# Rounded three-pass latent products, shared low parts and a reordered MLP norm in a hybrid GLA and MLA layer kernel

## The reference

```python
D_MODEL = SEQ = 1024; GLA_HEADS, GLA_DK, GLA_DV = 4, 64, 128; MLA_HEADS = 8; D_FF = 4096
h = _rmsnorm(x, attn_norm[l])
z = h @ w_in[l]
zq, zk, zv, zgate, zg, zcq, zckv, zkpe = jnp.split(z, split_pts, axis=-1)
gate_logit = (zgate @ w_gate_up[l] + b_gate[l]).astype(jnp.float32)
log_a = jnp.maximum(jax.nn.log_sigmoid(gate_logit) / GLA_GATE_NORMALIZER, GLA_LOG_GATE_MIN)
o_gla = _gla_chunked(gq, gk, gv, log_a)            # chunked scan, chunk 64
o_gla = _rmsnorm(o_gla, gla_out_norm[l]) * jax.nn.silu(zg)
q  = (_rmsnorm(zcq,  q_a_norm[l])  @ w_uq[l])      # 256 -> 8 heads x 96
kv = (_rmsnorm(zckv, kv_a_norm[l]) @ w_ukv[l])     # 128 -> 8 heads x 128
# head norms, rotary part of 32, block-causal softmax attention
x = x + jnp.concatenate([o_gla, o_mla], axis=-1) @ w_out[l]
h = _rmsnorm(x, mlp_norm[l])
x = x + jnp.square(jax.nn.relu(h @ w_up[l])) @ w_down[l]
```

## Time and profile before

| | us |
|---|---|
| median of 3 runs | 1159.03 (1159.02 to 1159.75) |
| the profiled execution | 1160.03 |
| its span in the trace | 1158.1 |
| PE busy | 1126.1 (97%) |
| DVE busy | 786.6 (68%) |
| POOL busy | 529.6 (46%) |
| ACT busy | 468.7 (40%) |

### The profile page before, as it was taken

The page is one execution under the profiler, slowest core; times in us unless marked ns, Lnnn a source line. Parts: engine busy times, 40 slices in busy tenths (PEclk is TensorE's granted clock), DMA queues, the critical chain, the costliest instruction groups (busy, mean ns, idle before and its releaser), DMA issues.

```text
span 1158.1 us, 15248 instructions
## 1 busy us (share of the span) xinstructions
PE 1126.1 (97%) x5582; PEld 899.3 (78%) x5582; DVE 786.6 (68%) x1092; ACT 468.7 (40%) x891; POOL 529.6 (46%) x429
## 2 busy tenths in 40 slices
PE   5999999999999999999999999999999999999998
PEld 5977677776766768887788888888887888888887
DVE  5575776637777772157488755775798888988863
ACT  5343544315565562056423223322434344344341
POOL 2352442514344363235844444444536565564562
PEclk9998999999999999999999999999999999999999
DMA  7332242372212114323334334331589784466642
GB/s 244 88 110 64 81 149 81 91 224 63 74 33 60 51 38 153 120 92 128 108 112 161 110 127 143 112 109 72 200 288 340 257 296 147 131 188 216 203 120 89
DMA packets 98346, 158.42 MB, mean 137 GB/s; under 512 B 9248, under 2 KB 38960, under 8 KB 98272
## 3 DMA queue, kind: packets, MB, share of 16 engines
q1 hardware_dynamic: 96720, 152.53, 40.0%
q10 hardware_dynamic: 1008, 3.67, 0.9%
q0 software_dynamic: 544, 1.24, 0.6%
HBM read 115.46 MB, written 41.94 MB: 136 GB/s over the span
## 4 chain that ended last, share of the span: by engine, by line
PE 83%; DVE 9%; issue 3%; POOL 2%; ACT 1%; DMA 1%; SPq 0%; ACTq 0%; DVEq 0%; POOLq 0%
PE ps L1808 78%; PE ps L2043 2%; PE ps L1880 1%; DVE g_cum L1375 1%; DVE t_all L1580 1%; DVE t_new L1580 1%; DVE dr_lo L1580 1%; POOL wi_lo L753 1%; DMA gain<-in_attn_norm_dram 1%; DMA up_raw<-in_w_up_dram 1%; PE ps L1823 0%; PE ps L1945 0%; DVE stage L1580 0%; DVE m_qk L1349 0%; DVE m_nm L1525 0%
## 5 line engine op out<-in xcount | busy, mean ns | idle before, releaser
L1808 PE MATMUL ps<-dr_hi,dl_hi 128*128 128x512 f32 x448 | 174.5, 390 | 1.6 <-DVE dr_lo L1580 1.6
L1808 PE MATMUL ps<-dr_hi,dl_lo 128*128 128x512 f32 x448 | 174.3, 389 | 0.0
L1808 PE MATMUL ps<-dr_lo,dl_hi 128*128 128x512 f32 x448 | 174.3, 389 | 0.0
L882 POOL TENSOR_TENSOR ua_lo<-up_raw,ua_hi 128x1024 fp32r<-128x1024 f32 x46 | 116.8, 2541 | 118.3 <-ACT ua_hi L918 118.3
L904 POOL TENSOR_TENSOR dl_lo<-l_raw,dl_hi 128x512 fp32r<-128x512 f32 x64 | 101.5, 1610 | 70.2 <-ACT dl_hi L918 69.8
L1808 PE MATMUL ps<-wi_hi,a_hi 128*128 128x512 f32 (+1 forms) x256 | 105.9, 414 | 5.3 <-POOL wi_lo L753 3.8
L1808 PE MATMUL ps<-a_hi,ua_hi 128*128 128x512 f32 x256 | 99.9, 390 | 2.0 <-ACT u_two L918 1.8
L904 POOL TENSOR_TENSOR dl_lo<-s_all,dl_hi 128x512 fp32r<-128x512 f32 x48 | 75.0, 1582 | 58.4 <-ACT dl_hi L918 57.7
L1808 PEld LDWEIGHTS ps<-dr_hi,dl_hi 128*128 128x128 f32 x448 | 84.1, 188 | 20.3 <-issue 2.8
L1808 PE MATMUL ps<-a_lo,ua_hi 128*128 128x512 f32 x256 | 99.6, 389 | 0.0
L1808 PE MATMUL ps<-a_hi,ua_lo 128*128 128x512 f32 x256 | 99.6, 389 | 0.0
(11 more groups left out here) (218 smaller groups left out, 2422.9 us busy)
## 6 DMA issues: line engine op xcount, KB each, us to landing
r_raw<-in_w_down_dram SPq DMA_DIRECT2D x144, 256.0 KB, 3.4
hidden<-stage SPq DMA_DIRECT2D x72, 256.0 KB, 2.1
up_raw<-in_w_up_dram SPq DMA_DIRECT2D x16, 1024.0 KB, 5.5
l_raw<-hidden SPq DMA_DIRECT2D x64, 256.0 KB, 3.3
raw<-in_w_in_dram SPq DMA_DIRECT2D x24, 256.0 KB, 3.0
z_gla<-z_stage SPq DMA_DIRECT2D x16, 256.0 KB, 2.0
raw<-in_w_out_dram SPq DMA_DIRECT2D x16, 256.0 KB, 6.7
xs<-in_x_dram SPq DMA_DIRECT2D x8, 512.0 KB, 7.2
```

The costliest lines, as they stand in the source:

```text
L882: pool.tensor_tensor(ua_lo[n % UP_RING][:, :, :], up_source(g, product), ua_hi[n % UP_RING][:, :, :].bitcast(F32), ALU.subtract).then_inc( ...
L1808: return pe.matmul(dst, lhsT, rhs, start=start, stop=stop, skip_group_check=onto)
```

## The change

1. The latents' factors are split too: `c_hi` is ACT's copy, `c_lo` a multiply-and-subtract of DVE (three of 128x128 per block); the weights `m_uq` (128x1536) and `m_ukv` (128x1024) get high parts from ACT and low parts from DVE once, around step 8. The products behind HEADS become three one-pass matmuls each.
2. START becomes 7, 9, ... 21: HEADS falls on odd steps, both transposes on even ones. The head transposes come five steps after START for all blocks, and GATE_T and LOGITS one step earlier.
3. The gates are worked in place in `g_cum`: the lower bound goes into the bias step, the absolute value and a subtraction are dropped, and the sums go behind steps 27 and 28.
4. DVE makes the low parts of tiles 3, 5 and 7 of groups 1 to 3, ahead of `tile_out` of the last step of the group before.
5. `m_ukv` is loaded later, behind the last tiles of group 1.
6. In the MLP norm POOL makes the root of position 4 and 6 ahead of T4's low part, the low parts of T1 to T3 one position later in its list, and `up_low(0, P5)` ahead of three low parts of the last position; ACT makes T4's last high part after `first_parts(1, P1)`.

```diff
-        START = [6, 8, 11, 13, 16, 18, 20, 22]
+        START = [7 + 2 * b for b in range(NB)]
-        HEADS_T_AT = [at_step + (6 if b < NB // 2 else 5) for b, at_step in enumerate(START)]
+        HEADS_T_AT = [at_step + 5 for at_step in START]
-        GATE_T, LOGITS = NB + 1, NB + 3
+        GATE_T, LOGITS, GATE_SUMS = NB, NB + 2, 3 * NB + 3
+        def low_by_vector(n):
+            return KT <= n < KT * IN_GROUPS and n % KT in (3, 5, 7)
+        def low_made(n):
+            of_vector = sum(low_by_vector(m) for m in range(n + 1))
+            return (wlo_done2, of_vector) if low_by_vector(n) else (wlo_done, n + 1 - of_vector)
...
 # SP
-                    sp.wait_ge(wlo_done, KT * q + k - RING + 1)
+                    sp.wait_ge(*low_made(KT * q + k - RING))
...
-                    sp.dma_start(m_ukv[:, :], w_ukv[0]).then_inc(mla_w_in, 16)
                 for b in range(NB - 1):
                     stores(NB * q + b)
                 if q + 1 < IN_GROUPS:
                     for k in range(RING + 2, KT):
                         in_piece(q + 1, k)
+                    if q == 0:
+                        sp.dma_start(m_ukv[:, :], w_ukv[0]).then_inc(mla_w_in, 16)
...
 # POOL
                         for k in range(0, 2) if b == 0 else range(2, KT):
-                            in_low_part(q + 1, k)
+                            if not low_by_vector(KT * (q + 1) + k):
+                                in_low_part(q + 1, k)
...
             for pos in range(NB):
+                if pos >= 2 and late(pos - 2):
+                    t_low(pos - 2, range(3))
                 pool.wait_ge(ssq_ready, NB + pos + 1)
                 rsqrt(rstd[:, 1, pos:pos + 1], ssq[:, 1, pos:pos + 1], D, rstd_ready)
-                if pos >= 1 and late(pos - 1):
-                    t_low(pos - 1, range(3 if pos == NB - 1 else 4))
+                if pos >= 2 and late(pos - 2):
+                    t_low(pos - 2, (3,))
+            t_low(NB - 2, range(3))
             pool.wait_ge(ulo_done, 2)
             up_low(1, P1)
             t_low(NB - 2, (3,))
             t_low(NB - 1, (0,))
             up_low(1, P2)
-            t_low(NB - 1, (1, 2))
             up_low(0, P5)
-            t_low(NB - 1, (3,))
+            t_low(NB - 1, (1, 2, 3))
...
 # ACT
-                        last = copy(m_cT[:, i, :], ps[:, 3, i * P:(i + 1) * P], ga[:, i:i + 1])
+                        last = copy(c_hi[:, i, :], ps[:, 3, i * P:(i + 1) * P], ga[:, i:i + 1])
-                    step(act.activation(g_cum[:, :, :], g_log[:, :, :], ACT.Abs))
...
                 behind(b)
+            act.wait_ge(mla_w_in, 32)
+            copy(m_uq_hi[:, :, :], m_uq[:, :, :]).then_inc(mla_hi, 1)
+            copy(m_ukv_hi[:, :], m_ukv[:, :]).then_inc(mla_hi, 1)
             for q in range(1, IN_GROUPS):
...
             for n, (g, product) in enumerate(UP_ORDER):
                 if product in (P1, P5) and n >= 1:
                     first_parts(g, product)
+                if n == 2:
+                    t_high(NB - 1, (3,))
...
-                if n == 1:
-                    t_high(NB - 1, (3,))
...
 # DVE
-                step(stt(g_log[:, t, :], g_log[:, t, :], 0.0, g_cum[:, t, :], ALU.min, ALU.subtract))
-                step(dve.tensor_scalar(g_log[:, t, :], g_log[:, t, :], 1.0 / GATE_NORM, LOG_GATE_MIN, ALU.mult, ALU.max))
+                step(dve.tensor_scalar(g_cum[:, t, :], g_cum[:, t, :], -1.0 / GATE_NORM, LOG_GATE_MIN, ALU.mult, ALU.max))
...
+                b = prep(s, LATENTS_T)
+                if b is not None:
+                    dve.wait_ge(cT_out, b + 1)
+                    for i in range(3):
+                        last = stt(c_lo[i][:, :], ps[:, 3, i * P:(i + 1) * P], ga[:, i:i + 1], c_hi[:, i, :].bitcast(F32),
+                                   ALU.mult, ALU.subtract)
+                    last.then_inc(clo_done, 1)
...
+            def in_low_parts(q):
+                for k in range(KT):
+                    n = KT * q + k
+                    if low_by_vector(n):
+                        dve.wait_ge(whi_done, n + 1)
+                        dve.tensor_tensor(wi_lo[:, n % SLICES, :], raw[:, k % RING, :], wi_hi[:, n % SLICES, :].bitcast(F32),
+                                          ALU.subtract).then_inc(wlo_done2, 1)
...
+                if b == NB - 1:
+                    in_low_parts(1)
                 tile_out(b)
                 behind(b)
...
             for s in range(NB, NB * IN_GROUPS - 1):
+                if s % NB == NB - 1:
+                    in_low_parts(s // NB + 1)
                 tile_out(s)
+                if s == NB:
+                    dve.wait_ge(mla_hi, 1)
+                    dve.tensor_tensor(m_uq_lo[:, :, :], m_uq[:, :, :], m_uq_hi[:, :, :].bitcast(F32), ALU.subtract)
+                    dve.wait_ge(mla_hi, 2)
+                    dve.tensor_tensor(m_ukv_lo[:, :], m_ukv[:, :], m_ukv_hi[:, :].bitcast(F32), ALU.subtract).then_inc(mla_lo, 1)
                 behind(s)
...
 # PE, behind HEADS
-                        pe.wait_ge(mla_w_in, 32)
+                        pe.wait_ge(mla_lo, 1)
+                        pe.wait_ge(gateT_out, 2)
-                    pe.wait_ge(cT_out, b + 1)
+                    pe.wait_ge(clo_done, b + 1)
                     for j in range(2):
+                        cols = slice(4 * j * DQK, 4 * (j + 1) * DQK)
                         for i in range(QR // P):
-                            mm(ps[:, 4 + j, 0:4 * DQK], m_cT[:, i, :], m_uq[:, i, 4 * j * DQK:4 * (j + 1) * DQK],
-                               i == 0, i == QR // P - 1)
+                            split_product(ps[:, 4 + j, 0:4 * DQK], c_hi[:, i, :], c_lo[i][:, :], m_uq_hi[:, i, cols],
+                                          m_uq_lo[:, i, cols], i == 0, i == QR // P - 1)
                     for j in range(2):
-                        last = mm(ps[:, 6 + j, :], m_cT[:, 2, :], m_ukv[:, j * W:(j + 1) * W], True, True)
+                        cols = slice(j * W, (j + 1) * W)
+                        last = split_product(ps[:, 6 + j, :], c_hi[:, 2, :], c_lo[2][:, :], m_ukv_hi[:, cols],
+                                             m_ukv_lo[:, cols], True, True)
```

More of the change, by code:

```diff
@@ L133, in layer @@
         m_ukv = at("m_ukv", [P, MH * (NOPE + MV)], 152 * KB)
-        m_cT = at("m_cT", [P, 3, P], 156 * KB)
+        m_uq_lo = at("m_uq_lo", [P, QR // P, MH * DQK], 146 * KB, F32R)
+        m_ukv_lo = at("m_ukv_lo", [P, MH * (NOPE + MV)], 152 * KB, F32R)
+        m_uq_hi = at("m_uq_hi", [P, QR // P, MH * DQK], 106 * KB, F32R)
+        m_ukv_hi = at("m_ukv_hi", [P, MH * (NOPE + MV)], 112 * KB, F32R)
+        c_hi = at("c_hi", [P, 3, P], 156 * KB, F32R)
+        c_lo = [at(f"c_lo{n}", [P, P], offset * KB // 2, F32R) for n, offset in enumerate((233, 239, 315))]
         q_stage = at("q_stage", [DQK, MH, P], 160 * KB)
@@ L285, in layer @@
         x2_stored = [sem(f"x2_stored{n}") for n in range(NB // 2)]
-        up_in = [sem(f"up_in{n}") for n in range(4)]
+        w_landed = [sem(f"w_landed{n}") for n in range(4)]
         sums_ready, uhi_done, ulo_done, part_ready = sem("sums_ready"), sem("uhi_done"), sem("ulo_done"), sem("part_ready")
@@ L292, in layer @@
         keep_stored, pairs_ready = [sem(f"keep_stored{n}") for n in range(2)], sem("pairs_ready")
-        s1_in, l_in, r_in = ([sem(f"{name}{n}") for n in range(4)] for name in ("s1_in", "l_in", "r_in"))
+        s1_in, l_in = ([sem(f"{name}{n}") for n in range(4)] for name in ("s1_in", "l_in"))
         d_sum, dlhi_done, drhi_done, dllo_done, drlo_done = (sem(name) for name in
@@ L391, in right_landed @@
             n = RIGHT_STEPS.index(t)
-            return r_in[n % 4], 16 * sum(raw_right(u) for u in RIGHT_STEPS[n % 4:n + 1:4])
+            return w_landed[n % 4], 16 * (2 * UG // 4 + sum(raw_right(u) for u in RIGHT_STEPS[n % 4:n + 1:4]))
         def left_source(t):
@@ L673, in down_load @@
                     for m, (k, half) in enumerate(tiles):
[L674 removed]
+                        sp.dma_start(right_raw(t, m), w_tile(f, k, half)).then_inc(w_landed[n % 4], 16)
             hidden_stores(0, (0, 1))
@@ L1395, in behind @@
                         dve.wait_ge(logit_ready, n + 1)
-                        dve.tensor_scalar(g_log[:, t, i * W:(i + 1) * W], ps[:, 4 + n, :], bg[:, t:t + 1], None,
-                                          ALU.add).then_inc(logit_out, 1)
-                if s - 3 - LOGITS in range(GT):
-                    gate_sums(s - 3 - LOGITS)
+                        dve.tensor_scalar(g_cum[:, t, i * W:(i + 1) * W], ps[:, 4 + n, :], bg[:, t:t + 1], LEAST_LOGIT,
+                                          ALU.add, ALU.max).then_inc(logit_out, 1)
+                if s - GATE_SUMS in range(GT):
+                    gate_sums(s - GATE_SUMS)
+                b = prep(s, LATENTS_T)
[5 more added lines that the diff above has]
+                    last.then_inc(clo_done, 1)
                 b = prep(s, HEAD_SUMS)
```

34 lines of the change are left out of this document (16 added, 18 removed).

## The result

The changed kernel takes 1169.21 us in the median of four executions (1167.89 to 1171.89), against 1159.03 for the kernel before: a ratio of 1.0094, 95% interval 1.0070 to 1.0117. The forecast was 1159.7 with a range of 1151 to 1164.5, so it is 9.5 us out, and the time lies above the range. The profiled execution took 1167.89 with a span of 1165.8.

The account below looks back on a forecast made before the run. PE's work (busy 97% of the span) plus its waits bounds the kernel. Input stage +2.2, clock +3.0 and MLP norm -4.5 sum to +0.7 on the median 1159.03, forecast 1159.7 us; range 1151 to 1164.5.

Parts of the forecast that it names:

- Part 1: Products behind HEADS: 3.45 us per block instead of 4.30, -6.8 us for eight blocks (bounds -3.6 and -7.1).
- Part 2: Input steps 16 and 24: sharing low parts removes waits for POOL, -6.1 us; moving the gate sums, -1.1.
- Part 3: Behind steps 16 and 22: DVE blocked on tile 7 delays head norms, PE waits 6.9 + 5.7 = +12.6 us.
- Part 4: Start, before the first HEADS: PE waits 0.4 at k = 7, 0.5 for latents' scaling, 2.7 for c_lo; +3.6 us.
- Part 6: MLP norm: most waits for xn and the one for u_two go, -4.5 us (bounds -3 and -5.3).
- Part 5: Granted clock: each of the two new long waits costs 1.5 us by a lower-clock stretch, +3.0 (0 to 6.8).
- rival 3: Behind steps 16 and 24: 6.8 us at half speed each, +3.8 over the forecast, 1163.5 us; chance 0.2.
- both chains at 8 and no clock: Lower end of the forecast case: DVE's two chains at their lower bound and no clock loss, given as 1155 us.

Follow-up runs that it names:

- e4: e2 with HEADS multiplied by plain float32 products as in the kernel before, the split parts still made but unused; 1159.57 us, ratio 1.0010.
- e5: Changed kernel with unused PE products filling three waits: ahead of the first HEADS and behind steps 16 and 24; 1159.68 us, ratio 1.0010.
- e1: Changed kernel with POOL making all low parts of the input weights again, none on DVE; 1158.34 us, ratio 0.9999.
- e8: e2 with the gate sums back behind steps 13 and 14 in place of steps 27 and 28; 1160.90 us, ratio 1.0018.
- e2: Changed kernel with DVE making the low parts of tiles 3 and 5 only, tile 7 left to POOL; 1157.08 us, ratio 0.9982.
- e6: Changed kernel with POOL's tile 2 low part moved ahead of the h_rs root of steps 14 and 22; 1164.33 us, ratio 1.0048.
- e3: Kernel before with the MLP norm's new order alone, nothing of the input stage; 1154.64 us, ratio 0.9965.
- e7: Changed kernel with DVE making tiles 3, 4, 5, first group's ahead of the rotary turns, and POOL's tile 2 ahead of the root; 1156.55 us, ratio 0.9987.
- e10: e5 without the unused products ahead of the first HEADS, only the waits behind steps 16 and 24 filled; 1165.97 us, ratio 1.0069.

## Why the prediction was wrong, by its steps

**Part 1, products (-6.8): right.** 3.49 us per block against 3.45; e4 gives 6.7 by the products' rows and 6.2 in the stage. Its lower bound was mis-stated: 384-column products at 0.23 would have left -1.4, not -3.6.

**Part 2, shared low parts (-6.1, -1.1): right in kind.** Steps 16 and 24 lost the waits of POOL's pace, but k = 6 of step 16 waited 2.2 and not 0.7, so that the step took 7.8 and not under 7. The load of its tile reached ACT 3.8 us after its issue at 135.46, where the term had 2.6 from the earlier trace rows. That SP issued two loads at once (135.46 and 135.85) isn't the reason: in e5 they are as close, and the first reached ACT after 2.6; in e1 they are 2.8 apart, and it took 3.8. What makes this load take 2.6 or 3.8 stays open. The gate sums' move was under-priced (e8: 3.4 to 4.9), and this was hidden in the same sum.

**Part 3, DVE blocked on tile 7 (+12.6): the mechanism right, the size low.** 7.8 and 6.0 from start to start, against 6.9 and 5.7, for the slower load and because two instructions of the head norms, not one, ran beside POOL's low parts (7.7 us for all). e2 and e6 show the cause from two sides.

The head norms of L1389 and L1390 beside POOL took 1.76 and 1.37, where instructions of the same shapes took 0.69 (L1388) and 0.41 (L1391) alone. The Trainium skill's page "SBUF — State Buffer", section "Who interferes with whom", has the two engines excluding each other for an instruction; by that rule the stretched rows are to be expected, and the trace agrees: each reads two tiles. The rotary turns of the earlier trace rows read one tile and a column of factors, so of those rows the prediction's sentence on this rule is borne out by L1349 alone.

**Part 4, the start (+3.6): right in size.** 0.6 at k = 7 (0.4), 0.2 for the latents (0.5), 3.5 for `c_lo` (2.7): 4.3.

**Part 6, MLP norm (-4.5): right.** 3.9 in this trace, 4.1 alone (e3).

At full clock the forecast was -2.3 against the kernel before, and +2.7 was measured. The 5.0 between them: 0.7 from part 4, 1.5 from k = 6, 1.2 from part 3, 0.3 from the eight HEADS, 0.6 from part 6, 0.3 ahead of step 8, 0.2 around the span, 0.2 not placed. Each is small and all have the same sign; together they are over half of the miss.

**Part 5, the clock (+3.0): the step that failed, with 4.5 of the 9.5 the largest single miss, in two ways.** In the profiled execution the clock cost 5.2 more than before. The stretches behind steps 16 and 24 cost 1.35 and 2.1, close to the term, though not by its reasoning: each lasted 6.8 us, as rival 3 had it, and was cheap because it began inside the wait; the gates' stretch stayed, as forecast; but no term stood for the down projection, which lost 1.7 with no change to its work. And the clock isn't one number: the forecast took it for a property of the kernel, read from one execution. The kernel before lies at 1.000 in nine of 30 executions, and its profiled one stood 1.0 above the median; the changed one never came above 0.990, and its profiled one stands 1.3 below its median. Together: 5.0 for waits and work, 2.2 for the clock in the profiled execution, 2.3 for how the two profiles stand to their medians: 9.5. With the waits filled (e5) the clock is back at the level of the kernel before. What was missing is that each further wait, the 3.4 us for `c_lo` among them, is a further chance for a stretch: e1, e6, e7 and e10 have one that begins within 1 us of its end, the changed kernel's profile has none there. Rival 3, slower by the lower clock after each wait, named the mechanism; its 1163.5 stopped short, as it had the forecast's waits and only two stretches. The sum's lower end was wrong too: both chains at 8 and no clock give 1152.1 and not 1155, which this result didn't put to use.

The Trainium skill's page "TensorE: Matmul & The Clock Gate", section "What's actually happening", says that an idle array falls to the lower clock and sustained work brings it back. By it, filling the waits should keep the clock up, and e5 shows this with 0.999.

## What to carry to other kernels

Where PE is 97% busy, a wait costs its length and often clock besides (here 20 us of waits and 8.6 of clock in one profile, 3.4 of it at the gates), so a forecast needs a term for each wait over a microsecond, and two kernels are compared by their time at full clock as well as by their medians. When low parts are shared between two engines, the one with other duties should take only those tiles whose data doesn't hang on the other's queue. An order that removes one engine's hold-up has to be followed through every queue: tile 2's earlier low part helped at step 16 and harmed at step 24, for one tanh that stood in between.

## What the runs showed of the hardware

- Filling waits with products that nobody uses made a kernel 9.5 us faster: its executions had a clock of 0.997 to 1.000 in place of 0.985 to 0.990.
- The same program had executions with a mean clock of 1.000 and of 0.997, at 1156.3 and at 1162.0 us; a single profile shows one of these.
- The same wait of 1.36 us in the down projection was followed by a clock of 0.50 in the changed kernel and in e5, and by 1.00 in e3 and e10.
- The stretches of 0.50 behind steps 16 and 24 of the changed kernel began inside the wait and cost 1.35 and 2.1 us, though they lasted 6.8 us each.
- The same load of 256 KB, issued 0.4 us ahead of the next, reached ACT after 3.8 us in the changed kernel and in e10, and after 2.6 in e5 and 2.7 in e4.
